# Order of the attention stage, place of the bias load and pace of the convolution products in a two-layer encoder kernel

## The reference, cut to what matters

```
h = rmsnorm(x, norm_mix[i]);  proj = h @ w_in[i]
q, k, v, cglu, sc_b, sc_c, sc_h, gates = split(proj)
# attention, 16 heads, 4 of keys and values, chunks of 64 positions; a chunk sees itself and the one before
logits = q.k / 8 + bias(rel_table);  probs = softmax([logits, sink])[..., :-1];  y_a = (probs @ v) @ w_attn_out[i]
# convolution module, 31 taps per channel, causal
c = causal_dwconv(ca * sigmoid(cb), conv_dw[i]) + conv_dw_bias[i]
y_b = silu(layernorm(c)) @ w_conv_out[i]
# short gated convolution, 3 taps
y_c = (sc_b * causal_dwconv(sc_c * sc_h, sc_conv[i])) @ w_sc_out[i]
x = x + (g0 * y_a + g1 * y_b + g2 * y_c) @ w_mix_out[i]        # g = sigmoid(gates)
```

## Time and profile before

| | us |
|---|---|
| median of 3 runs (lowest, highest) | 1177.83 (1177.38, 1177.88) |
| the profiled execution's own time | 1177.76 |
| its span in the profile | 1176.0 |
| TensorE busy | 1136.9 (97%) |
| VectorE busy | 821.8 (70%) |
| ScalarE busy | 704.3 (60%) |
| GpSimd busy | 425.2 (36%) |

### The profile page before, as it was taken

The page is one execution under the profiler, slowest core; times in us unless marked ns, Lnnn a source line. Parts: engine busy times, 40 slices in busy tenths (PEclk is TensorE's granted clock), DMA queues, the critical chain, the costliest instruction groups (busy, mean ns, idle before and its releaser), DMA issues.

```text
span 1176.0 us, 24193 instructions
## 1 busy us (share of the span) xinstructions
PE 1136.9 (97%) x9340; PEld 1121.9 (95%) x9340; DVE 821.8 (70%) x1217; ACT 704.3 (60%) x1139; POOL 425.2 (36%) x405
## 2 busy tenths in 40 slices
PE   6998999998999999999999999999999999999996
PEld 5998999997999999999989999999999999999996
DVE  6786887775766665456699887878776675545657
ACT  5477887764745543444667788876574455434454
POOL 0288668795002000002127886679620200000012
PEclk9998999998999999999999999999999999999998
DMA  8554434444454456455335553435545535645541
GB/s 308 211 194 164 144 109 146 172 166 154 171 195 169 161 196 228 152 179 202 139 126 193 203 180 108 144 123 200 179 173 195 199 125 213 212 153 190 198 144 37
DMA packets 29358, 201.54 MB, mean 171 GB/s; under 512 B 3521, under 2 KB 3713, under 8 KB 5841
## 3 DMA queue, kind: packets, MB, share of 16 engines
q1 hardware_dynamic: 27648, 195.38, 46.9%
q0 software_dynamic: 1088, 4.74, 1.2%
q10 hardware_dynamic: 528, 0.15, 0.1%
HBM read 199.19 MB, written 3.69 MB: 173 GB/s over the span
## 4 chain that ended last, share of the span: by engine, by line
PE 69%; POOL 11%; ACT 8%; DVE 5%; DMA 3%; issue 3%; POOLq 0%; ACTq 0%; DVEq 0%; SPq 0%
PE bank L324 21%; PE bank L326 21%; PE bank L325 21%; POOL pacc L1314 10%; ACT w_hi L553 3%; DMA w_raw<-in_wstream 3%; DVE w_lo L890 2%; ACT cprod L553 1%; POOL sqsum L1325 1%; PE bank L436 1%; PE bank L361 1%; PE bank L362 1%; ACT cv L742 1%; PE bank L364 1%; POOL cv L1314 1%
## 5 line engine op out<-in xcount | busy, mean ns | idle before, releaser
L324 PE MATMUL bank<-h_hi,w_hi 128*128 128x256 f32 x1856 | 533.1, 287 | 3.1 <-DVE w_lo L890 1.7
L325 PE MATMUL bank<-h_lo,w_hi 128*128 128x256 f32 x1856 | 526.7, 284 | 0.0
L326 PE MATMUL bank<-h_hi,w_lo 128*128 128x256 f32 x1856 | 526.6, 284 | 0.0
L890 DVE TENSOR_TENSOR w_lo<-w_raw,w_hi 128x2048 fp32r<-128x2048 f32 x183 | 429.0, 2346 | 111.3 <-ACT w_hi L553 110.9
L553 ACT ACTIVATE w_hi<-w_raw 128x2048 fp32r<-128x2048 f32 (+1 forms) x185 | 351.1, 1900 | 164.0 <-DMA w_raw<-in_wstream 127.1
L324 PEld LDWEIGHTS bank<-h_hi,w_hi 128*128 128x128 f32 x1856 | 357.6, 193 | 10.6 <-issue 6.8
L325 PEld LDWEIGHTS bank<-h_lo,w_hi 128*128 128x128 f32 x1856 | 357.8, 193 | 0.2
L326 PEld LDWEIGHTS bank<-h_hi,w_lo 128*128 128x128 f32 x1856 | 357.6, 193 | 0.0
L1314 POOL TENSOR_TENSOR pacc<-pacc,cprod 128x256 f32<-128x256 f32 x280 | 308.4, 1102 | 82.8 <-ACT cprod L553 45.0
L324 PE MATMUL bank<-act_hi,w_hi 128*128 128x256 f32 x1024 | 292.3, 285 | 4.5 <-DVE w_lo L937 2.9
L325 PE MATMUL bank<-act_lo,w_hi 128*128 128x256 f32 x1024 | 290.8, 284 | 0.0
(11 more groups left out here) (139 smaller groups left out, 860.9 us busy)
## 6 DMA issues: line engine op xcount, KB each, us to landing
w_raw<-in_wstream SPq DMA_DIRECT2D x183, 1024.0 KB, 4.8
rel_bias_rows<-rel_bias_by_distance POOLq DMA_DIRECT2D x1, 2560.0 KB, 17.6
bias<-rel_bias_rows POOLq DMA_DIRECT2D x1, 1536.0 KB, 10.6
xs<-in_x SPq DMA_DIRECT2D x2, 512.0 KB, 4.4
w_raw<-in_wstream SPq DMA_DIRECT2D x2, 512.0 KB, 7.8
out_y<-xs SPq DMA_DIRECT2D x4, 256.0 KB, 2.6
zacc<-in_p POOLq DMA_DIRECT2D x2, 256.0 KB, 4.4
prms<-in_prm SPq DMA_DIRECT2D x1, 328.0 KB, 10.5
```

The costliest lines, as they stand in the source:

```text
L324: nc.tensor.matmul(o, wh, hi, start=first, stop=False, skip_group_check=True)
L325: nc.tensor.matmul(o, wh, lo, start=False, stop=False, skip_group_check=True)
L326: return nc.tensor.matmul(o, wl, hi, start=False, stop=last, skip_group_check=True)
L890: nc.vector.tensor_tensor(w_lo[:, n % RING, :], w_raw[:, n % RAW_RING, :], f32(w_hi[:, n % RING, :]), ALU.subtract).then_inc(lo_ready, 1)
```

## The change

Five edits. In layer 0, `conv_products` gets the same counts as in layer 1. In ScalarE's list of the attention stage, round_attn goes ahead of the weight rounding and exponentials(j) ahead of copy_probs(j-1). In VectorE's list softmax(j) goes ahead of low_attn(j-3), and the work on strips is done one chunk later (`branch_strips(j-1)` in chunk j, ahead of w_lo; the last chunk's at the end). GpSimd issues the bias load ahead of the fifteenth add of its first tile, and masks it behind that tile. No instruction is added or left out.

```diff
-                        conv_products(CGLU_PRODUCTS * (t if L else max(1, t - 3)))
-                before_qkv, qkv_products = (CGLU_PRODUCTS * (DT - 1), QKV_PRODUCTS) if L else (CGLU_PRODUCTS * (DT - 4), QKV_PRODUCTS + 1)
-                before_sc = before_qkv + qkv_products * (KT + QT // 2)
+                        conv_products(CGLU_PRODUCTS * t)
+                before_qkv = CGLU_PRODUCTS * (DT - 1)
+                before_sc = before_qkv + QKV_PRODUCTS * (KT + QT // 2)
...
-                        conv_products(before_qkv + qkv_products * (s // 2 + 1))
+                        conv_products(before_qkv + QKV_PRODUCTS * (s // 2 + 1))
...
                 for j in range(C0["attn_out"] - C0["sc"]):
-                    after_chunk(C0["sc"] + j - 1)
                     if 0 <= j - 3 < QT:
                         round_attn(j - 3)
+                    after_chunk(C0["sc"] + j - 1)
+                    if j < QT:
+                        exponentials(j)
                     if 0 <= j - 1 < QT:
                         copy_probs(j - 1)
...
-                    if j < QT:
-                        exponentials(j)
                     conv_products(before_sc + SC_PRODUCTS * (j + 1))
...
+                def branch_strips(j):
+
                     for s in (2 * j, 2 * j + 1):
...
+                for j in range(C0["attn_out"] - C0["sc"]):
+                    if j == 0:
+                        dve.wait_ge(bias_ready, 2)
+                    if 0 <= j - 2 < QT:
+                        normalise(j - 2)
+                    if j < QT:
+                        softmax(j)
+                    if 0 <= j - 3 < QT:
+                        low_attn(j - 3)
+                    if 0 <= j - 1 < QT:
+                        denominators(j - 1)
+                    if j > 0:
+                        branch_strips(j - 1)
+                    after_chunk(C0["sc"] + j - 1)
+                branch_strips(C0["attn_out"] - C0["sc"] - 1)
                 low_sc(DT - 1)
...
+            def load_bias():
+
+                pool.wait_ge(rel_stored, 32)
+                pool.dma_start(bias[:, :, :], skewed).then_inc(bias_in, 16)
+
+            def mask_bias():
+
+                pool.wait_ge(bias_in, 16)
+                nc.gpsimd.memset(bias[0:CHUNK, :, P:KEYS], NEG_INF).then_inc(bias_ready, 1)
+                pool.wait_ge(bias_ready, 1)
+                nc.gpsimd.memset(bias[CHUNK:P, :, 0:CHUNK], NEG_INF).then_inc(bias_ready, 1)
+                pool.wait_ge(bias_ready, 2)
...
                         n = b * CONV_WIDTH + k
+                        if L == b == 0 and k == CONV_WIDTH // 2:
+                            load_bias()
                         pool.wait_ge(prod_ready, L * PRODUCTS + n + 1)
...
+                    if L == b == 0:
+                        mask_bias()
```

More of the change, by code:

```diff
@@ L1291, in _ @@
                            ).then_inc(rel_stored, 16)
-            pool.wait_ge(rel_stored, 32)
             skewed = bass.AP(tensor=rel_rows.tensor, offset=P - 1, ap=[[REL - 1, P], [P * REL, N_HEADS], [1, KEYS]])
[L1295 to L1301, removed]
+            def load_bias():
[7 more added lines that the diff above has]
+                pool.wait_ge(bias_ready, 2)
             pool.wait_ge(dve_set, 1)
```

## The result

The changed kernel takes 1170.87 us (median of 5 runs, 1170.58 to 1173.36) against 1177.83: faster by 6.96 us, ratio 0.9946 with an interval of 0.9931 to 0.9960. Forecast were 13.1 us. The profiled execution has a span of 1168.8 us, 7.2 less than before.

A forecast was written before the change was run, and what follows sets the result against it. TensorE was taken as the bound, busy nearly everywhere except for a few waits and the clock losses behind them. Terms -16.7 + 1.0 + 3.2 + 0 - 0.6 = -13.1 us gave 1164.7 us, range 1159.5 to 1172.0.

The forecast's parts named there:

- The reading by pairs of layers: Equal TensorE points compared across layers: layer 0 loses 16.7 us against layer 1, all regained with layer 1's product counts.
- the two long ones: TensorE's long waits: L491 on GpSimd's channel sum, 5.8 us, and L421, first scores, on VectorE's last tap, 4.25 us.
- The attention stage's order on ScalarE: Exponentials ahead of copies delay the first L447: +1.6 us per layer, +3.2 in all; bounds -0.9 and +2.5 per layer.
- a rival, at 0.20: TensorE's clock falls in the longer first L447 wait, 2.5 us a time: 1167.2, with both layers 1169.7; chance 0.20.
- in between the trace decides nothing: The clock fell in a 4.25 us wait, not in one of 1 us; for lengths between, the trace was called undecided.
- The bias in the middle of tile 0: GpSimd's later bias issue and memsets, 3.3 us if not covered, delay ScalarE through the ring: +1.0 taken, bounds 0 and +3.3.
- at most as much again, and less to nothing: Bias transfer near 58 us, competing with a w_raw load: costs TensorE at most the earlier 1.45 us, or less to nothing.
- L436's waits: TensorE's two waits for act_lo at L436 go because round_attn comes first: -0.6 us, bounds 0 and -0.9.
- VectorE's order: Softmax ahead of low_attn, strips one chunk later: value 0, bounds -0.5 and +0.5 us for each of sixteen chunks.
- Reordering does what it is for: Rival: first attention-stage copies come in time in both layers, -1.8 in place of +3.2: 1159.7 us; chance 0.12.
- the ScalarE-bound stage: Rival: a TensorE-VectorE-ScalarE loop within each attention-stage chunk adds 1 us in each of sixteen: 1180.7 us; chance 0.07.
- L491 stays: Rival: with only 1.3 us in hand, L491's wait partly returns, half of 8.6 us: 1169.0 us; chance 0.05.

The follow-up runs named there:

- experiment 7, pace_only: The kernel before with only the even pace of products in layer 0; bias load and mask as before: 1170.08 us, ratio 0.9939.
- experiment 1, copy_before_exp: The changed kernel with copy_probs(0) moved ahead of exponentials(1) in chunk 1 of the attention stage: 1164.70 us, ratio 0.9882.
- experiment 3, old_orders: The changed kernel with ScalarE's and VectorE's attention-stage orders as before; even pace and new bias place kept: 1164.74 us, ratio 0.9886.
- experiment 4: The kernel before with only the new attention-stage orders of ScalarE and VectorE; pace and bias as before: 1184.52 us, ratio 1.0052.
- experiment 5: The changed kernel with exponentials(j) back in mid-chunk on ScalarE and copy_probs(0) first in chunk 1: 1160.12 us, ratio 0.9854.
- experiment 6: The kernel of experiment 5 with VectorE's attention-stage order also back as in the kernel before: 1160.97 us, ratio 0.9848.
- copy_first: The changed kernel with copy_probs(0) ahead of both the weight rounding and exponentials(1) in attention-stage chunk 1: 1164.42 us, ratio 0.9887.
- mask_gap: The kernel of experiment 5 with the bias mask's memsets ahead of GpSimd's add 24 of tile 0, not behind the tile: 1159.31 us, ratio 0.9844.

## Why the prediction was right or wrong

**The reading by pairs of layers was right**, and with it the largest term. Layer 0 had lost 16.71 us against layer 1; the change brought 4.01 + 2.31 + 5.94 + 2.07 = 14.33 of them at the four places foreseen, before what it gave back. Not foreseen was which edit pays for what: the pace alone removes L491's loss (experiment 7). In the reading of the waits, "the two long ones" leaves out two at the start, of 7.9 us at 7.90 (L389) and of 2.9 us at 12.06 (L324); all kernels here have them, and they change nothing in the sum.

**Where it failed: "The attention stage's order on ScalarE", which put the longer wait of the first L447 at +1.6 us per layer and gave the clock behind it no term.** The wait was sized fairly (+2.30 and +1.29, together 3.6 against 3.2). The half clock was left to a rival, at 0.20, because the trace of before showed it behind waits of 4.25 and 5.78 us and not behind ones of 1. (The same trace has one wait in between, 1.59 us between the layers, with the clock at 1.00; "in between the trace decides nothing" holds only above that.) It fell in both layers, 3.08 + 1.52 = 4.60 us. That rival, "with both layers 1169.7", is what happened (1170.87). Experiments 1, 3, 4 and 5 show that the order is the cause: without it the wait is short and the time 6 us less, with the order alone the old kernel loses 6.9. Of the clock they show that in layer 1 it stays up with the shorter wait; in layer 0 a half clock of half the length is left in experiments 1 and 3 and none in 5.

The terms close the account. From the forecast of -13.1, +4.60 for the half clocks, +0.39 for the waits of L447, +1.38 since layer 0 won 14.33 where the sum had 15.71 (16.71 less the 1.0 for GpSimd), -0.36 at L436 and -0.09 at the end give -7.18; the last mark stands at -7.19.

**"The bias in the middle of tile 0"** had the size, 1.0 taken and 1.7 found, and the wrong cause. The sum laid it to GpSimd's 3.3 us of issue and memsets. At the memsets the distance between the layers does not fall further in the changed kernel (572.88 at the w_lo of chunk 11, 572.90 at chunk 13); the transfer that I had put "at most as much again, and less to nothing" made one w_raw load 1.62 us late for ScalarE, and GpSimd's full ring kept the delay up to the scores. Of the changed kernel, GpSimd and VectorE:

```profile
81.76 0.95 POOL L1310 MEMSET bias<- 64x1024 f32 x1
82.79 1.29 POOL L1327 TENSOR_TENSOR pacc<-cprod 128x256 f32<-128x256 f32 x1
...
81.20 2.28 DVE L890 TENSOR_TENSOR w_lo<-w_raw,w_hi 128x2048 fp32r<-128x2048 f32 x1
```

The memset inside the w_lo takes 0.95 us as it did alone; the add behind it takes 1.29 us instead of 0.75 and ends 0.6 us behind w_lo. By the Trainium skill ("SBUF — State Buffer", section "Who interferes with whom"), a VectorE instruction with two inputs in SBUF contends with a GpSimd instruction that reads SBUF, not with one that only writes it. The trace agrees, by this 0.95.

**L436's waits** went, -0.96 with what followed against -0.6, by the cause named. **VectorE's order** at value 0 was right as far as experiment 6 can tell. **"Reordering does what it is for"**, at 0.12, and the ScalarE-bound stage, at 0.07, did not come: L447 to L447 the pitch in the middle is 8.85 us as before. **"L491 stays"**: it has gone; L495, the second channel mean, waits 0.7 us in layer 0 instead, which no step of mine had.

## What to carry to other kernels

Where a kernel does the same work twice, subtract the starts of equal points: each fall of the difference is a loss with a place. A wait put in front of TensorE costs its length and may cost the clock behind it, so price both, also where the same trace shows a shorter wait that cost nothing. Doing first what is on the longest chain pays only if it is needed next: here exponentials got a lead of a whole chunk, and the copies, which TensorE needed now, paid for it in the first chunks of the stage.

## What the runs showed of the hardware

The length of the wait alone does not tell whether the clock falls. It fell to 0.50 behind waits of L447 of 3.12, 2.63, 2.48, 2.02, 1.41 and 1.40 us and behind waits of the first scores of 2.16 and 1.85. It stayed at 1.00 behind the scores' waits of 1.74 and 1.62, behind copy_first's second L447 with 1.66, behind pace_only's first L447 with 1.40, and in every kernel here behind a wait of 1.6 us between the layers, of which this is the one of the kernel before:

```profile
599.80 0.39 PE L324 MATMUL bank<-act_hi,w_hi 128*128 128x256 f32 x1 [1.59 <-DVE act_lo L927]
```

So the same wait of 1.40 us at the same L447 cost the clock in one kernel and not in another. Where it fell it stayed low for 3.4 or 6.8 us; the stretches that the table and experiment 1 price cost 1.5 and 3.1 us. What else decides was not found.

Runs of one kernel spread over 5 us for copy_first and copy_before_exp, and over 0.7 us for mask_gap, which waits 1.16 us at the scores and not at L447. In copy_first the mean granted clock goes with the time, from 0.998 in the fastest run to 0.994 in the two slowest. That such waits widen the spread is likely from this but not shown: old_orders, with the same wait of 1.4 us as copy_before_exp, spreads over 2.1 us.

GpSimd's issue of the bias load took 1.19 us beside a w_lo that began with it, no longer than before:

```profile
57.54 1.19 POOL L1303 DMA_DIRECT2D bias<-rel_bias_rows  x1
...
57.60 2.29 DVE L890 TENSOR_TENSOR w_lo<-w_raw,w_hi 128x2048 fp32r<-128x2048 f32 x1 [0.96 <-ACT w_hi L553]
```
